# Prompt scores straight from the projected q and k tiles, in plain float32 on 32 and 64 partitions

## The reference

```
qa, ka, va, ga, xb, gb, qc, kc, vc, gc = split(rms_norm(x) @ w_in)     # x: 1024 x 1024, w_in: 1024 x 3072
A: 4 heads, q and k in two halves of 32:   sc[c] = q[c] . k[c] * 32**-0.5, causal, c = 0, 1
   p = softmax(sc[0]) - lam * softmax(sc[1]);  a_core = p @ v
B: b_core = RG-LRU(causal conv of width 4 over xb)
C: 4 heads of 64: three dilated windows, merged by their softmax denominators,
   which is one softmax over all keys with log(count) added to the score;  c_core = p @ v
y = concat(rms_norm(a_core) * silu(ga), b_core * silu(gb), c_core * silu(gc)) @ w_out
out = x + rms_norm(y)
```

## Time and profile before

| | |
|---|---|
| time, median of 3 runs | 907.91 us (904.59 to 911.07) |
| the profiled execution | 908.83 us; span of its profile 907.0 us |
| busy share of the span | PE 78%, DVE 57%, ACT 37%, POOL 31% |
| mean granted TensorE clock | 0.874 of full speed |
| moved by DMA | 148.46 MB, mean 164 GB/s |

### The profile page before, as it was taken

How to read it: one execution, slowest core, us unless ns; L and a number is a source line. 1 busy time by engine, 2 the same in 40 slices (tenths; PEclk the granted TensorE clock), 3 DMA queues, 4 the chain that set the end, 5 groups by cost and what they waited for, 6 DMA issues and landing times.

```text
span 907.0 us, 11603 instructions
## 1 busy us (share of the span) xinstructions
PE 707.5 (78%) x4192; PEld 567.7 (63%) x4192; DVE 514.9 (57%) x845; ACT 337.6 (37%) x729; POOL 284.2 (31%) x195
## 2 busy tenths in 40 slices
PE   5699999998599888985168723777467369979996
PEld 4699998887588767774035412454355256668885
DVE  5747774443575678653268821795825488664222
ACT  6522322322122312211037712766628366662111
POOL 4135455564154445551023201511141362000000
PEclk9599999999699989998559865888959589999999
DMA  8645778775896857765544433331314261413221
GB/s 243 209 144 142 216 235 276 222 273 164 282 296 204 300 187 282 259 230 188 167 141 142 165 106 108 112 104 67 109 59 151 82 189 45 71 1 116 96 96 67
DMA packets 87278, 148.46 MB, mean 164 GB/s; under 512 B 14131, under 2 KB 57955, under 8 KB 87222
## 3 DMA queue, kind: packets, MB, share of 16 engines
q1 hardware_dynamic: 68790, 80.60, 28.7%
q0 software_dynamic: 18432, 67.12, 22.2%
HBM read 124.47 MB, written 23.26 MB: 163 GB/s over the span
## 4 chain that ended last, share of the span: by engine, by line
PE 55%; DMA 21%; DVE 8%; SPq 6%; ACT 5%; issue 4%; POOL 2%; ACTq 0%; DVEq 0%; POOLq 0%
PE ps L1773 9%; PE ps L1775 8%; PE ps L1774 8%; DMA ka_d<-KL 7%; PE ps L1834 4%; DMA TMP<-gate_d 4%; PE ps L1906 3%; PE ps L1907 3%; PE ps L1908 3%; DMA v_c<-out 3%; PE ps L1818 3%; DMA stack<-ka_d 2%; PE ps L1725 2%; DMA kc<-in_w_out 2%; SPq L565 2%
## 5 line engine op out<-in xcount | busy, mean ns | idle before, releaser
L1773 PE MATMUL ps<-xh,wh 128*128 128x344 f32 x576 | 198.0, 344 | 2.7 <-DVE xl L1216 1.5
L1774 PE MATMUL ps<-xl,wh 128*128 128x344 f32 x576 | 187.8, 326 | 0.0
L1775 PE MATMUL ps<-xh,wl 128*128 128x344 f32 x576 | 187.6, 326 | 0.0
L1773 PEld LDWEIGHTS ps<-xh,wh 128*128 128x128 f32 x576 | 111.2, 193 | 24.6 <-issue 21.3
L1774 PEld LDWEIGHTS ps<-xl,wh 128*128 128x128 f32 x576 | 111.8, 194 | 0.0
L1775 PEld LDWEIGHTS ps<-xh,wl 128*128 128x128 f32 x576 | 111.7, 194 | 0.0
L1801 PE MATMUL ps<-stack,stack 128*128 128x512 f32 (+3 forms) x96 | 37.0, 473 | 89.4 <-DMA stack<-ka_d 64.9
L770 POOL DMA_INDIRECT vbuf<-in_cache_a_v,index x64 | 62.8, 981 | 137.8 <-PE ps L1725 128.5
L762 POOL DMA_INDIRECT kbuf<-in_cache_a_k,index x64 | 77.2, 1206 | 75.7 <-DVE sc L1275 65.4
L1273 DVE TENSOR_TENSOR prod<-kbuf,qrep 128x1024 f32<-128x1024 f32 x64 | 79.2, 1237 | 36.6 <-DMA kbuf<-in_cache_a_k,index 35.8
L1403 DVE CUSTOM_DVE_ANT_0 T<-ps,mask_a 128x128 f32<-128x128 f32 (+7 forms) x64 | 46.0, 753 | 88.2 <-ACT E L1036 46.7
(11 more groups left out here) (262 smaller groups left out, 1182.4 us busy)
## 6 DMA issues: line engine op xcount, KB each, us to landing
wraw<-in_w_in SPq DMA_DIRECT2D x24, 512.0 KB, 5.7
gate_d<-passing SPq DMA_DIRECT2D x8, 516.0 KB, 6.4
TMP<-gate_d SPq DMA_DIRECT2D x8, 516.0 KB, 8.0
xraw<-in_x_prompt SPq DMA_DIRECT2D x8, 512.0 KB, 6.0
out<-nat SPq DMA_DIRECT2D x8, 512.0 KB, 4.7
stack<-kc_d SPq DMA_DIRECT2D x8, 512.0 KB
kc<-in_w_out SPq DMA_DIRECT2D x8, 512.0 KB, 12.1
x_res<-in_x_prompt SPq DMA_DIRECT2D x8, 512.0 KB, 3.9
```

What stands on the lines that cost most here:

```text
L1773: pe.matmul(pr, wh[t % 2][:, kt, :], xh[:, kt, cols], start=(kt == 0), stop=False)
L1774: pe.matmul(pr, wh[t % 2][:, kt, :], xl[:, kt, cols], start=False, stop=False)
L1775: ins = pe.matmul(pr, wl[t % 3][:, kt, :], xh[:, kt, cols], start=False, stop=(kt == KT - 1))
```

## The change

The splits, the DRAM scratch of q and k and the stacks go. `scores` reads the projected tiles: for A, half c of head h lies on 32 partitions from 64 * (h % 2) + 32 * c, for C head h on 64 partitions from 64 * (h % 2); both operands are plain float32. For A, the loop over the two halves is now inside the loop over blocks of 512 keys, so that matmuls of the two halves take turns, and both PSUM areas are waited for before the first of them. `wo_raw` gets a place of its own where the stacks were (it lay on kc0 and kc1), so that the first two loads of output weights wait for nothing.

```diff
-        stack = [[at(f"stack{s}{i}", [P, S], F32R) for i in range(4)] for s in range(2)]
+        wo_raw = [at(f"wo_raw{i}", [P, D]) for i in range(2)]
...
-        wo_raw = [tile_of[f"kc{i}"][:, 0:D] for i in range(2)]
...
-            def store_pair(p, e):
...
-                if step - 10 in SPLIT_AT and SPLIT_AT.index(step - 10) % 2:
-                    store_pair(0, SPLIT_AT.index(step - 10) // 2)
...
-            def load_stack(hh, c0=0, c1=S, arrived=None):
...
             def load_wo(k):
-                if k < 2:
-                    sp.wait_ge(split_done, 16)
-                else:
+                if k >= 2:
                     sp.wait_ge(wol_done, k - 1)
...
-            load_stack(0, 0, FIRST, first_stack)
             sp.dma_start(mask_a[:], a["c_mask_a"]).then_inc(mask_in, 16)
-            load_stack(0, FIRST, S)
             gates_stored(sp)
             sp.dma_start(v_a[:], nat_out["va"]).then_inc(va_in, 16)
-            load_stack(1)
             sp.dma_start(mask_c[:], a["c_mask_c"]).then_inc(late_in, 16)
             for u in range(NU + 1):
                 h, q = UNITS[u] if u < NU else (8, 0)
-                if q == NQ - 1 and h in (0, 2, 4):
-                    store_pair(h // 2 + 1, 0)
-                    store_pair(h // 2 + 1, 1)
-                if q == 1 and h >= 1 and h + 1 < 8:
-                    load_stack(h + 1)
                 if u == UNITS.index((HA, 2)):
                     sp.wait_ge(scored, ITEM_NO["s", UNITS.index((HA, 1)), 0] + 1)
-                    sp.wait_ge(split_done, 8)
                     sp.dma_start(v_c[:], nat_out["vc"]).then_inc(vc_nat_in, 16)
...
-            def split_pair(p, i):
...
-                if step in SPLIT_AT:
-                    split_pair(0, SPLIT_AT.index(step))
...
-                act.wait_ge(split_done, 4 * (h // 2 + 1))
                 act.activation(d[r:r + 64, q * P:(q + 1) * P], ps[r:r + 64, RB, 128:256],
                                ACT.Copy).then_inc(core_out, 1)
...
             def scores(u):
                 h, q = UNITS[u]
                 w = (q + 1) * P
-                sl = stack[h % 2]
-                if u == 0:
-                    pe.wait_ge(first_stack, 16 * 4)
-                if u == FIRST // P or (q == 0 and h >= 1):
-                    pe.wait_ge(stack_in[h % 2], stacked(h))
-                for c in range(2 if h < HA else 1):
-                    it = ("s", u, c)
-                    keep_free(pe, it)
-                    out = score_bank(it)
-                    for k0 in range(0, w, 512):
-                        k1 = min(w, k0 + 512)
-                        if h < HA:
-                            ins = pe.matmul(out[:, k0:k1], sl[2 * c][:, q * P:(q + 1) * P], sl[2 * c + 1][:, k0:k1],
-                                            start=True, stop=True)
-                        else:
-                            pe.matmul(out[:, k0:k1], sl[0][:, q * P:(q + 1) * P], sl[1][:, k0:k1], start=True, stop=False)
-                            ins = pe.matmul(out[:, k0:k1], sl[0][:, q * P:(q + 1) * P], sl[2][:, k0:k1],
-                                            start=False, stop=True)
-                    ins.then_inc(scored, 1)
+                n, d = (2, DKA) if h < HA else (1, DHC)
+                tq = tile_of[("qa0", "qa1", "qc0", "qc1")[h // 2]]
+                tk = tile_of[("ka0", "ka1", "kc0", "kc1")[h // 2]]
+                for c in range(n):
+                    keep_free(pe, ("s", u, c))
+                for k0 in range(0, w, 512):
+                    k1 = min(w, k0 + 512)
+                    for c in range(n):
+                        r = 64 * (h % 2) + d * c
+                        ins = pe.matmul(score_bank(("s", u, c))[:, k0:k1], tq[r:r + d, q * P:(q + 1) * P], tk[r:r + d, k0:k1],
+                                        start=True, stop=True)
+                        if k1 == w:
+                            ins.then_inc(scored, 1)
```

More of the change, by code:

```diff
@@ L378, in build @@
         acc_zero = sem("acc_zero")
-        split_done = sem("split_done")
         scored = sem("scored")
@@ L438, in build @@
         EARLY_MIX = 2
[L439 to L445, removed]
         def keep_free(eng, it):
@@ L634, in _ @@
             sp.wait_ge(proj, ALL_CHUNKS)
-            def load_stack(hh, c0=0, c1=S, arrived=None):
[L638 to L652, removed]
-                else:
-                    r = DHC * (hh % 2)
-                    sp.dma_start(sl[0][:].bitcast(F32), qc_d[p - 2, hh % 2].rearrange("g r n -> (g r) n")).then_inc(arrived, 16)
-                    for g in range(2):
-                        k = kc_d[p - 2, g, r:r + DHC, :].unsqueeze(0).to_broadcast([2, DHC, S])
-                        sp.dma_start(sl[1 + g][:].bitcast(F32), k).then_inc(arrived, 16)
             def load_wo(k):
-                if k < 2:
-                    sp.wait_ge(split_done, 16)
-                else:
+                if k >= 2:
                     sp.wait_ge(wol_done, k - 1)
-                sp.dma_start(wo_raw[k % 2], w_out[k]).then_inc(wo_in[k % 2], 16)
-            load_stack(0, 0, FIRST, first_stack)
+                sp.dma_start(wo_raw[k % 2][:], w_out[k]).then_inc(wo_in[k % 2], 16)
             sp.dma_start(mask_a[:], a["c_mask_a"]).then_inc(mask_in, 16)
-            load_stack(0, FIRST, S)
             gates_stored(sp)
             sp.dma_start(v_a[:], nat_out["va"]).then_inc(va_in, 16)
-            load_stack(1)
             sp.dma_start(mask_c[:], a["c_mask_c"]).then_inc(late_in, 16)
@@ L789, in _ @@
                 load_v(m)
-            def split_pair(p, i):
-                if p == 0 and i == 0:
-                    for j in range(2):
-                        pool.wait_ge(nat_out_done[j], 16 * 4)
-                    pool.wait_ge(evac, 3 * (TI["ka0"] + 1))
-                if p == 0 and i == 2:
-                    pool.wait_ge(kc_used, NB)
-                    pool.wait_ge(job, JOB_NO["cpv", NB - 1, 0] + 1)
-                if p >= 1 and i == 0:
-                    pool.wait_ge(qk_out, stored(p - 1))
-                src = tile_of[(("qa0", "qa1", "qc0", "qc1"), ("ka0", "ka1", "kc0", "kc1"))[i // 2][p]][:, 0:S]
-                high, low = ((QH, QL), (KH, KL))[i // 2]
-                if i % 2 == 0:
-                    pool.tensor_copy(high[:], src).then_inc(split_done, 1)
-                else:
-                    pool.wait_ge(split_done, 4 * p + i)
-                    pool.tensor_tensor(low[:], src, high[:].bitcast(F32), ALU.subtract).then_inc(split_done, 1)
             for step in range(PSTEPS):
@@ L816, in _ @@
                 sample_events(step)
-                if step in SPLIT_AT:
-                    split_pair(0, SPLIT_AT.index(step))
             for u in range(NU):
-                h, q = UNITS[u]
-                if 4 <= q and h in (0, 2, 4):
-                    split_pair(h // 2 + 1, q - 4)
                 sample_events(PSTEPS + 2 * u)
@@ L1139, in split_wo @@
                     act.wait_ge(attended, HA * NQ)
-                    act.wait_ge(qk_out, stored(3))
+                    for i in range(2):
+                        act.wait_ge(nat_out_done[i], 16 * 4)
                 act.wait_ge(wo_in[k % 2], 16 * (k // 2 + 1))
-                act.activation(wo[k][:, 0, :], wo_raw[k % 2], ACT.Copy).then_inc(woh_done, 1)
+                act.activation(wo[k][:, 0, :], wo_raw[k % 2][:], ACT.Copy).then_inc(woh_done, 1)
             stage1_over(act)
```

23 lines of the change are left out of this document (1 added, 22 removed).

## The result

The changed kernel takes **843.23 us** (median of 5 runs, 842.17 to 851.23) against 907.91 for the kernel before beside it: ratio 0.9302, 95% interval 0.9265 to 0.9339. The forecast was 855.0 and the range 832 to 893. The profiled execution is the longest of the five, 851.23 us with a span of 849.4, so the trace shows 57.6 us of the gain (907.0 - 849.4) where the medians show 64.7.

What follows compares the result with a forecast made beforehand. No engine bounds the attention throughout: VectorE is nearest in A, TensorE at the end of C, with stops between put down to stack and gate waits. 907.0 - 78 + 24 = 853 us span, plus 1.8, gives 855 us; range 832 to 893.

Steps and rivals of the forecast that it cites:

- The start: Start of attention: first scores no longer held, first attend at 441 us instead of 463.3; gain 22 us (19 to 27).
- v_a is what is late next: Start of attention: the first attend waits for v_a, landing between 436 and 444 us; only scores and maxima run ahead.
- Stack wait and stop: TensorE's 2.9 us stack wait goes, gain 3 us; the stop at 527 us shrinks, gain 28 of 31 us.
- the waits name the cause: Attention: the stops come from TensorE's 64.9 us of stack waits and GpSimd's 82.6 us of gate tile waits.
- v_c and the output weights: In C: v_c's 15.1 us stall shrinks by 9 us (0 to 15), ScalarE's 14.5 us w_out wait by 10.
- The rival that transfers stay slow: v_a, v_c and w_out load as slowly as before, gate tiles keep 8 us: 882 us, chance 0.12.
- GpSimd's splits: During attention: VectorE instructions beside a split took 2.47 us instead of 1.22; removing twelve splits gains 6 us, at most 15.
- A's dearer passes: A's plain float32 scores add 16.5 us of TensorE work with halves overlapping; 11 us of it shows.
- C's: C's plain float32 scores add 16.5 us: 7 us paid in full at the end, 6 of the other 9.5.
- The sum: Whole span: gains of 78 us, 24 us added (7 to 33), so 907.0 becomes 853 us of span.
- The overlap: A's scores: two halves on different partitions run at once, a 512-key pair in about 1 us, not 1.9.
- the rival without it: A's halves don't overlap: A adds 50.4 us instead of 16.5, 23 more exposed; 878 us, chance 0.18.

Runs made afterwards that it cites:

- Experiment 2: Kernel before with the new score matmuls; splits, stores and stack loads still issued, but TensorE waits for no stack: 924.15 us, ratio 1.0129.
- experiment 3: Two kernels: changed kernel with GpSimd's sixteen splits put back, results unused, 846.43 us; the same plus SyncE's waits for splits and scores, without their DMAs, 844.67 us.
- experiment 8's first kernel: Changed kernel with C's units in head pairs, the score matmuls of two heads issued alternately: 848.70 us, ratio 0.9361.
- experiment 1: Changed kernel with both score halves of an A head read from the same 32 rows, so they can't overlap: 900.58 us, ratio 0.9865.
- experiment 9: Extra 256-column matmul ahead of each A score pair from unit 4: 843.17 us on the changed kernel, 835.05 on head pairs with late waits and early v_c.

## Why the prediction was right

By its own steps, against the stages under the table:

*The start*: 22 predicted (19 to 27), 26.5 measured. v_a was taken at 441 us, by its old landing; it landed in 5.4 us, below even the lower bound of 7.8, at 430.4 us, and nothing waited for it. So the step that v_a is what is late next did not come true: the first attend ran 6.4 us after v_a's landing, in its place behind the scores and transposes of the first units.

*Stack wait and stop*: 3 + 28 predicted. The stop gave 29.4; the small wait is part of the stretch up to unit 15. The size was right and the reason half right. The prediction wrote that "the waits name the cause: TensorE waited 64.9 us in four waits for the stacks". Experiment 2 takes these waits away and nothing is gained, because a chain through a gate load behind the same transfers ended last, 4.6 us after the stack wait, in the kernel before too. The prediction read the waits and not that chain, which the trace of before already held. The gain came because the transfers themselves went.

*v_c and the output weights*: 9 + 10 predicted, 7.4 + 12.2 measured. The rival that transfers stay slow because sizes and rows are unchanged is refuted by the landings of 5.4, 5.8 and 3.4 us. The new place of `wo_raw` was not run alone, so its share of the 12.2 us is not known. These differences also hold C's dearer passes between the units.

*GpSimd's splits*: 6 predicted; with and without them the times differ by nothing measurable (experiment 3). So this gain is not seen. VectorE's time beside them is real (9.3 us), but it was priced as if VectorE still set the pace after the change.

*A's dearer passes*: 11 exposed predicted. The trace of after shows 2.5 lost up to unit 15, which with the small wait's 3 us makes 5.5, and 6.6 from unit 16 to 32: 12. That agreement is luck of the profiled execution, the longest of the five. It took 87.6 us from unit 16 to 32; experiment 8's first kernel, whose code in A is the same, took 78.5 (its clock in A was 0.83 in place of 0.77), experiment 3's two kernels 78.8 each, and the kernel before 81.0. So nearer to the median this stretch lost nothing and gained some 2.5 us, and A's passes cost about 3 us, not 11. The working rested on VectorE being ahead of TensorE in A by 36.3 to 32.5 us. Over the whole free stretch of the kernel before the two were nearly level:

```profile
463.00:527.00 64.00, 52.66 (x279) 31.59 (x278) 54.17 (x102) 41.82 (x95) 19.81 (x14) 0.81 0.43 148
```

*C's*: 13 predicted, 9.5 measured from unit 47 on; what was lost before that is inside the differences for v_c and the output weights.

*The sum*: 54 us of span predicted, 57.6 measured on the trace, and 64.7 by the medians. The forecast of 855.0 was 11.8 us too high. The largest differences are A's term, too dear by about 8 us, and the start, too small by 4.5; the splits' 6 went the other way.

*The overlap*: taken, and right: 1.06 us for a pair, close to the 0.94 of one matmul. The Trainium skill, "TensorE: Matmul & The Clock Gate", Part 3, which says that operands in different groups of 32 rows run at once, agrees with it: 1.88 / 1.06 = 1.8 for two. What was mis-sized is the rival without it. It was put at 23 us by two thirds exposed at full clock; experiment 1 gives 51: the extra passes were exposed in full, at a clock of 0.66 to 0.74.

## What to carry to other kernels

When one queue carries bulk transfers and the loads that engines wait for, look at the queue's own time from issue to issue before counting waits: here, removing a wait or moving one load handed the loss to the next load in it. Where two waits end together, neither is worth its own length; ask for each what would end next. And plain float32 on row slices is cheap only if two matmuls on different rows are issued one after the other; check with a kernel that puts both on the same rows.

## What was not expected of the hardware

The granted clock stayed at 0.50 (1.2 GHz) while the profile shows TensorE busy all the time. Windows of the changed kernel in A:

```profile
526.00:530.00 4.00, 2.11 (x8) 0.95 (x8) 3.12 (x8) 3.20 (x6) 0.00 (x0) 0.82 0.46 133
530.00:534.00 4.00, 4.00 (x22) 2.40 (x22) 3.80 (x7) 2.66 (x5) 2.35 (x1) 0.50 0.00 0
534.00:538.00 4.00, 4.00 (x14) 1.89 (x13) 1.86 (x4) 2.56 (x5) 0.00 (x0) 0.50 0.47 136
```

Before the clock fell, TensorE had been busy for 2.11 of 4 us, with one wait of 2.16 us for a maximum of VectorE. It was busy without a gap from 528 us on, at 0.50 until 548, and the clock was back at 1.00 from 550 us. What ran meanwhile were scores of 32 rows, transposes and attends of 64 columns; why the clock stayed down so long is open (experiment 9). And a load of 516 KB landed 17.2 us after its issue with the stack traffic around it (experiment 2), one store of K's low part 28.0; the same gate loads took 4.2 us in the quiet queue of the changed kernel.
